# Scores of the last 32 tokens from gathered rows of expert_u, narrower score matmuls, and a rearranged end of the run, in one layer with product-key experts

## What is computed

```python
mix = token_mixer(x, w_in, sb_norm_w, ret_norm_w, w_out)
x = layer_norm(DEEPNORM_ALPHA * x + mix, ln1_w, ln1_b)
# experts: 8 heads, two lists of 128 keys each, the best 16 of 128*128 experts per head and token
expert_idx, gate = ...                         # (256, 8, 16)
u = jnp.take(expert_u, idx_b, axis=0)          # rows of 2048
act = gelu(einsum('thkd,td->thk', u, xb))      # one score per picked expert
v = jnp.take(expert_v, idx_b, axis=0)
ffn = einsum('thkd,thk->td', v, gate * act)
x = layer_norm(DEEPNORM_ALPHA * x + ffn, ln2_w, ln2_b)
```

## Time and profile before

| | before |
|---|---|
| median of 3 runs | 1876.7 us |
| the profiled execution | 1876.2 us |
| its span | 1874.4 us |
| TensorE busy | 1850.5 us, 99% |
| TensorE weight loads | 1572.4 us, 84% |
| VectorE busy | 1280.2 us, 68% |
| GpSimd busy | 1055.0 us, 56% |
| ScalarE busy | 1018.8 us, 54% |
| mean granted TensorE clock | 0.996 |

### The profile page before, as it was taken

The page is one execution under the profiler, slowest core; times in us unless marked ns, Lnnn a source line. Parts: engine busy times, 40 slices in busy tenths (PEclk is TensorE's granted clock), DMA queues, the critical chain, the costliest instruction groups (busy, mean ns, idle before and its releaser), DMA issues.

```text
span 1874.4 us, 30301 instructions
## 1 busy us (share of the span) xinstructions
PE 1850.5 (99%) x9326; PEld 1572.4 (84%) x9326; DVE 1280.2 (68%) x1886; ACT 1018.8 (54%) x1842; POOL 1055.0 (56%) x769
## 2 busy tenths in 40 slices
PE   9999999999999999999999999999999999999996
PEld 7888888888888888888888888887888888888885
DVE  4555676768565454555555557966898888888887
ACT  4455555545566565555555555555555555555553
POOL 0000231200488989788888887726888666665423
PEclk9999999999999999999999999999999999999998
DMA  7777776664655666788998888977999999999993
GB/s 246 236 240 224 230 239 204 184 204 160 217 170 181 194 186 203 200 192 196 246 230 195 194 192 273 294 232 259 360 390 359 391 338 358 395 375 370 378 341 91
DMA packets 202730, 476.42 MB, mean 254 GB/s; under 512 B 63504, under 2 KB 65744, under 8 KB 201840
## 3 DMA queue, kind: packets, MB, share of 16 engines
q1 hardware_dynamic: 131824, 391.56, 62.0%
q0 software_dynamic: 52416, 80.02, 15.8%
q10 hardware_dynamic: 18432, 4.20, 1.1%
HBM read 453.41 MB, written 21.07 MB: 253 GB/s over the span
## 4 chain that ended last, share of the span: by engine, by line
PE 96%; DVE 2%; DMA 1%; ACT 0%; POOL 0%; issue 0%; SPq 0%; ACTq 0%; DVEq 0%
PE ps L750 25%; PE ps L503 14%; PE ps L505 14%; PE ps L504 14%; PE ps L756 13%; PE ps L790 6%; PE ps L791 6%; PE ps L720 0%; DMA x_nat<-in_x 0%; PE ps L493 0%; DMA act_dram<-halves 0%; DVE stats L1779 0%; PE ps L554 0%; DVE ps L1776 0%; DVE y_out L1801 0%; DVE act_both L1263 0%
## 5 line engine op out<-in xcount | busy, mean ns | idle before, releaser
L750 PE MATMUL ps<-act_both,split_hi 128*128 128x512 f32 x2048 | 513.3, 393 | 0.0
L1059 ACT ACTIVATE split_hi<-raw 128x512 fp32r<-128x512 f32 x512 | 308.0, 625 | 292.2 <-PE ps L756 289.9
L750 PEld LDWEIGHTS ps<-act_both,split_hi 128*128 128x128 f32 x2048 | 368.6, 189 | 65.6
L1509 DVE TENSOR_TENSOR split_lo<-raw,split_hi 128x512 fp32r<-128x512 f32 x368 | 284.0, 788 | 201.7 <-ACT split_hi L1059 197.0
L1179 ACT ACTIVATE v_hi<-v_tile 128x1024 fp32r<-128x1024 f32 x248 | 263.2, 1062 | 254.4 <-PE ps L791 247.0
L1729 DVE TENSOR_TENSOR v_lo<-v_tile,v_hi 128x1024 fp32r<-128x1024 f32 x248 | 308.1, 1265 | 79.1 <-ACT v_hi L1179 78.9
L1250 DVE TENSOR_TENSOR split_lo<-raw,split_hi 128x512 fp32r<-128x512 f32 x304 | 232.5, 771 | 162.1 <-ACT split_hi L846 161.1
L846 ACT ACTIVATE split_hi<-raw 128x512 fp32r<-128x512 f32 x344 | 216.4, 631 | 226.7 <-PE ps L505 224.4
L1927 POOL DMA_INDIRECT gate_dram<-pick_n,places x192 | 300.3, 1564 | 59.4 <-issue 59.4
L1975 POOL DMA_INDIRECT rows<-in_expert_v,picked x128 | 208.4, 1629 | 189.3 <-DVE row_sum L1741 116.7
L756 PEld LDWEIGHTS ps<-act_both,split_lo 128*128 128x128 f32 x2048 | 279.6, 190 | 19.9
(11 more groups left out here) (206 smaller groups left out, 2131.8 us busy)
## 6 DMA issues: line engine op xcount, KB each, us to landing
raw<-in_expert_u SPq DMA_DIRECT2D x256, 512.0 KB
v_tile<-in_expert_v SPq DMA_DIRECT2D x256, 512.0 KB, 7.0
raw<-in_w_in SPq DMA_DIRECT2D x112, 512.0 KB
raw<-in_w_out SPq DMA_DIRECT2D x32, 512.0 KB
...
act_dram<-halves ACTq DMA_DIRECT2D x128, 32.0 KB
```

The source lines that it names most:

```text
L750: return nc.tensor.matmul(ps[:, bank, :], split_hi[:, q % SPLITS, i * P:(i + 1) * P], act_both[:, k, :, :].rearrange("p a t -> p (a t)"), ...
L1059: nc.scalar.activation(split_hi[:, q % SPLITS, :], raw[:, q // 2, q % 2, :], ACT.Copy).then_inc(hi_ready, 1)
L1509: vec.tensor_tensor(split_lo[:, q % SPLITS, :], raw[:, q // 2 % RAWS, q % 2, :], split_hi[:, q % SPLITS, :].bitcast(f32), ALU.subtract).th ...
```

## The change

Five things change together.

1. The last 32 tokens (`OWN`) leave the dense scores. The score matmuls run over `UT` = 224 columns: `wide` over 2 x 224, `narrow` over 224. `act_dram` keeps 32 columns.
2. Their scores come from gathered rows: 32 indirect DMAs (`load_u_row`), each bringing 128 rows of `expert_u` of 8 KB, into two slots that lie in the space of the later value units. GpSimd issues two before the scatter, then one after every sixth scatter from the 25th on, the last two after it. VectorE computes one row's dot product per pair in pairs 22 to 53, in two halves of 1024 columns (`dot`), each between the splits of that pair, against the tokens' own activations (`x1_own`, read back from DRAM by SP). ScalarE applies the gelu before pair 62; GpSimd moves the results into place (`move_dots`).
3. The value stage's picked rows come in one indirect DMA of 8 KB per row; the weighing moves from GpSimd to VectorE (`weigh`, `weigh_dots`).
4. `PREFETCH` goes from 30 to 55, with a wait for all dots before it, and `APPLIED_AHEAD` from 48 to 32.
5. The end of the run: the last two weight tiles are split early into buffers of their own (`wlast`), the DMA of `row_sum`'s half is issued by GpSimd, and the norms of PART are reordered between VectorE, ScalarE and GpSimd.

```diff
+OWN = HB // 2
+UT = DENSE + OWN
+DOT_SLOTS, DOT_AT = 2, 22
+DOTS = OWN * PKEYS // P
-PREFETCH = 30
+PREFETCH = 55
-APPLIED_AHEAD = 48
+APPLIED_AHEAD = 32
...
@@ SP
-            with sp.Fori(1, PREFETCH) as i:
+            with sp.Fori(1, DOT_AT - 1) as i:
                 u_pair(i)
-            sp.wait_ge(picked_in, 64)
+            sp.wait_ge(picked_in, 128)
             sp.wait_ge(topk_done, 2)
+            sp.wait_ge(x1_out, X1_OUT)
+            for g in range(4):
+                sp.dma_start(x1_own[OWN * g:OWN * g + OWN, :], x1_dram[P - OWN:P, PART, :]).then_inc(own_in, 16)
+            with sp.Fori(DOT_AT - 1, PREFETCH) as i:
+                u_pair(i)
+            sp.wait_ge(dot_used, 2 * DOTS)
...
@@ TensorE, wide and narrow
-                    return nc.tensor.matmul(ps[:, bank, :], split_hi[:, q % SPLITS, i * P:(i + 1) * P],
-                                            act_both[:, k, :, :].rearrange("p a t -> p (a t)"), start=k == 0,
-                                            stop=k == KT - 1)
+                    return nc.tensor.matmul(ps[:, bank, 0:2 * UT].rearrange("p (a t) -> p a t", a=2),
+                                            split_hi[:, q % SPLITS, i * P:(i + 1) * P], act_both[:, k, :, 0:UT],
+                                            start=k == 0, stop=k == KT - 1)
...
-                    return nc.tensor.matmul(ps[:, bank, 0:SEQ], split_lo[:, q % SPLITS, i * P:(i + 1) * P],
-                                            act_hi[:, k, :], start=False, stop=False)
+                    return nc.tensor.matmul(ps[:, bank, 0:UT], split_lo[:, q % SPLITS, i * P:(i + 1) * P],
+                                            act_hi[:, k, 0:UT], start=False, stop=False)
...
@@ ScalarE, before split_w(PAIRS - 2)
+            act.wait_ge(applied, PAIRS)
+            for i in range(2):
+                nc.scalar.activation(wlast[i][:, HID:HID + HB], wexp[:, NT - 2 + i, P:DENSE], ACT.Copy)
+                nc.scalar.activation(wlast[i][:, HI0:HI0 + DENSE], wexp[:, NT - 2 + i, 0:DENSE], ACT.Copy
+                                     ).then_inc(last_w_hi, 1)
...
@@ VectorE
+            def dot(j, slot, half):
+
+                cols = slice(half * UNIT, half * UNIT + UNIT)
+                part = u_slots[slot][:, cols]
+                vec.scalar_tensor_tensor(out=part, in0=part, scalar=1.0, in1=x1_own[:, cols], op0=ALU.mult, op1=ALU.mult,
+                                         accum_out=dots[:, half, bass.ds(j, 1)]).then_inc(dot_used, 1)
+
+            def u_pair(pair, parity, j=None):
 
                 for k in (2, 3):
                     split_two(pair, parity, k)
+                    if j is not None and k == 2:
+                        dve.wait_ge(u_row_in[parity], pair * 8 - (DOT_AT + parity) * 8 + 16)
+                        dot(j, parity, 0)
                 add_halves(pair, 0, 2 * parity)
                 for k in (4, 5):
                     split_two(pair, parity, k)
+                    if j is not None and k == 4:
+                        dot(j, parity, 1)
...
-                chain.add(vec.tensor_scalar(places_f[HB:P, 1, :], places_f[HB:P, 0, :], 2.0, 1.0, ALU.mult, ALU.add))
                 dve.wait_ge(v_chain, chain.n)
-                chain.step(vec.tensor_scalar(places_f[HB:P, 0, :], places_f[HB:P, 0, :], 2.0, None, ALU.mult))
...
             dve.wait_ge(x1_out, X1_OUT)
-            dve.wait_ge(picked_in, 64)
-            with dve.Fori(PAIRS_A // 2, PAIRS // 2 - 1) as i:
+            dve.wait_ge(picked_in, 128)
+            with dve.Fori(PAIRS_A // 2, DOT_AT // 2) as i:
                 for s in range(2):
                     u_pair(i * 2 + s, s)
+            dve.wait_ge(own_in, 64)
+            with dve.Fori(DOT_AT // 2, (DOT_AT + DOTS) // 2) as i:
+                for s in range(2):
+                    u_pair(i * 2 + s, s, i * 2 + (s - DOT_AT))
...
@@ VectorE, value stage
+            def weigh(k):
+
+                part = slice(k * W_GROUP, (k + 1) * W_GROUP)
+                dve.wait_ge(act_in[k % 2], 16 * W_GROUP * (k // 2 + 1))
+                for half in range(2):
+                    some = slice(half * HB, half * HB + OWN)
+                    vec.tensor_tensor(picked_w[some, part], picked_act[some, part], picked_gate[some, part], ALU.mult
+                                      ).then_inc(weight_ready, 1)
...
@@ VectorE, end
-            for q in range(2):
-                end_norm(PART, q)
             for q in range(1, 4):
                 summed(FULL, q)
             end_var(FULL)
+            end_norm(PART, 0)
             end_shift(FULL)
...
@@ GpSimd
+                    def load_u_row(j):
+
+                        if j >= DOT_SLOTS:
+                            pool.wait_ge(dot_used, 2 * (j - DOT_SLOTS) + 2)
+                        eng.indirect_dma_start(u_slots[j % DOT_SLOTS][:, :], None, u_v,
+                                               bass.IndirectOffsetOnAxis(ap=dot_rows[:, j:j + 1], axis=0)
+                                               ).then_inc(u_row_in[j % DOT_SLOTS], 16)
+
+                    def rows_at(h, b, k):
+
+                        n = h * sum(per_head) + b * TOPK + k - h * TOPK
+                        j = DOT_SLOTS + (n - 24) // 6
+                        return j if n >= 24 and n % 6 == 0 and j < DOTS else 0
+
...
+                            if rows_at(h, b, k):
+                                load_u_row(rows_at(h, b, k))
...
+                    for g in range(4):
+                        eng.dma_start(dot_rows[OWN * g:OWN * g + OWN, :],
+                                      places_u[P - OWN:P, 0, DOTS * g:DOTS * g + DOTS]).then_inc(picked_in, 16)
...
-                    pool.wait_ge(picked_in, 64)
+                    pool.wait_ge(picked_in, 128)
...
+                    for j in range(DOT_SLOTS):
+                        load_u_row(j)
...
+                    for j in range(DOT_SLOTS + (PH * sum(per_head) - 24) // 6, DOTS):
+                        load_u_row(j)
...
                     load_row(STEPS - 1)
+                    pool.wait_ge(row_used, STEPS)
+                    eng.dma_start(row_half[0:HB, :], row_sum[HB:P, :]).then_inc(half_moved, 16)
```

122 lines of the change are left out of this document (78 added, 44 removed).

## The result

The changed kernel takes 1938.5 us (median of 4 runs, 1930.5 to 1946.4) against 1876.6 us (1876.0 to 1881.9) of the kernel before measured beside it: a ratio of 1.032 with an interval of 1.028 to 1.037. The forecast was 1881 us in a range up to 1908; the result is 57.5 us slower than the forecast and lies outside the range. The profiled execution was the slowest of the four: it took 1946.4 us, 8 us over the median, its span is 1944.3 us and its mean granted clock 0.972.

What follows compares the result with a forecast made beforehand. The prediction took TensorE, 96% of the span, to bound the kernel. Score stage +8.9, value stage +2 and end -6.4 us made +4.5 on 1876.2: 1881 us, with a range of 1862 to 1908.

Steps and rivals of the forecast that it cites:

- what a matmul costs: Score stage: narrower matmuls at 0.202 us wide and 0.112 us narrow, so a pair takes 10.05 us instead of 11.18.
- Rival C: Score matmuls: under 256 columns a matmul is no longer a single pass, some 2400 us in all; chance 0.05.
- Pairs 0 to 17: Early score stage: GpSimd's eight low halves, 10.24 us, set the pace, so 16.7 us are gained instead of 20.
- the mechanism: Score stage: late u rows hold VectorE, then TensorE; value stage starts at 1280.6 us, 8.9 later than before.
- Rival A: Score stage: the u rows keep up and TensorE sets the pace, 1805 us in all; chance 0.06.
- The stall of pair 18: Score stage: VectorE's longer wait for picked_in costs TensorE about 1.5 us, hidden since the rows set the end.
- the length of a scatter: GpSimd in the score stage: 1.873 us per scatter, six 11.24, with a row's 1.65 a cycle of 12.9 us.
- Rival B: Score stage: VectorE's dots slow GpSimd's scatter stream, a cycle of 15.3 us and 1946 us in all; chance 0.09.
- the start: GpSimd in the score stage: DMAs begin about 739 us, first scatter at 753.3, row 2 follows at 800.1.
- gate products beside splits: GpSimd's gate products beside VectorE's splits: VectorE at 9.6 us per pair; with weighing charged +2 us, 0 to 6.
- value stage: Value stage: TensorE busy throughout, one row gather issue instead of two; weighing and gate products together charged +2 us.
- the end: End of the run: early last weights gain 5.1 us, moved norms 2.9, new waits cost 1.3; together -6.4 us.

Runs made afterwards that it cites:

- experiment 1: Changed kernel with a u row gathered after every fourth scatter instead of every sixth: 1877.8 us, ratio 0.999 to the kernel before.
- experiment 3: Changed kernel with the u rows gathered but no dots, SP waiting for the rows themselves before the tile of pair 55: 1895.2 us, ratio 1.008.
- experiment 2: Changed kernel without gathered u rows and without dots: 1837.5 us, ratio 0.976.
- 7: Changed kernel with VectorE's low-half splits from pair 18 on subtracting a bank of PSUM instead of SBUF: 1904.7 us, ratio 1.013.
- 8: Changed kernel with the tokens' own activations copied to PSUM, so each dot reads one operand from SBUF: 1923.5 us, ratio 1.024.
- experiment 6: Changed kernel with the softmax reciprocals in PSUM, one operand of the multiplication that took 11.56 us: 1945.2 us, ratio 1.034.
- experiment 9: Changed kernel with eight gate products before the value stage instead of 32, and the dots moved before them: 1922.2 us, ratio 1.023.
- experiment 11: Kernel before with part 5 of the change alone (early last weights, row_sum's half on GpSimd, reordered norms): 1876.1 us, ratio 0.9992.
- 10: Changed kernel with a row every fourth scatter, eight gate products ahead, dots moved before them, picked_in wait behind pair 21: 1835.2 us, ratio 0.974.
- 12: Changed kernel with rows every fourth scatter, eight gate products ahead, dots moved early and in PSUM, picked_in wait and activation load later: 1826.4 us, ratio 0.972.

## Why the prediction was wrong

**Right: what a matmul costs.** 10.09 us a pair against 10.05 to 10.1, and the narrow products are 0.110 us apart (taken: 0.112). Rival C, that they are no single pass, is refuted. Pairs 0 to 17 are not paced by GpSimd, though the forecast assumed it: its low halves come every 1.25 us when nothing interrupts them, eight in 10.0, and 16 of the 17 steps from pair 1 to pair 17 are 10.09. From the start of pair 0 to that of pair 18 it took 185.3 us where the forecast had 187.1.

**Right: the mechanism.** The rows are late, VectorE waits for them with the splits behind it, and TensorE with VectorE. Rival A, that the rows keep up, would have needed experiment 1's rhythm: even with nothing beside it GpSimd's cycle is 12.5 us (experiment 3). The stall of pair 18 was hidden, though it was 7.6 us and not the 1.5 of the text, and the falls of the clock behind gaps seem to have been hidden too: the rows set the pace at a clock of 0.89 as well.

**Wrong: the length of a scatter, 27.8 us of 65.4.** The step that failed is "A scatter takes 1.873 us, six take 11.24", the larger term of the cycle of 12.9 us: 1.873 was read from a stretch in which pairs take 11.18 us, and carried over unchanged to one where VectorE has dots in addition and the splits come in another rhythm. A scatter took 1.729 + 0.305 = 2.034 us from start to start. Six are 12.2 instead of 11.24, and a row 1.71 instead of 1.65: 13.9. Over 27 cycles the scatters are 26.1 us of this and the rows 1.6. Rival B named this mechanism and priced it at a cycle of 15.3; it gave it to the dots alone. That its 1946 us comes close to the measured time is luck: the cycle brought 27.8 of its 65 us, and the others came from terms that it doesn't have. Splits and dots share it: the mean is 1.709 us without dots (experiment 2), 1.641 with the splits' second operand in PSUM (7), 1.681 with the dots' (8). The bounds "12.5 to 13.5" were drawn around one row's uncertainty, that of the row issue, and left the larger term, six scatters, without any.

Why the same splits lengthened the scatters so little before is a matter of when they meet. A scatter is lengthened if a VectorE instruction with two SBUF operands is already running when it starts, by what that instruction has left, less 0.13 us. In the changed kernel 86 of the 192 scatters started so and took 1.938 us on average; the other 106 took 1.560, none over 1.58. The rows follow the same rule: 30 of 32 started under one and took 1.43 us, the other two 0.98. In the kernel before the splits that ran into a scatter's start in the steady stretch had only 0.18 us left and the scatter took 1.59 us; further on 0.23 us and 1.64. So 1.564 was the mean of a favourable phase that came with the rhythm of 11.18 us, and no price of a scatter.

**Wrong: the start, 8.6 us until row 2.** The first scatter was 3.4 us late. GpSimd's DMAs began at 744.3 us, not 739: VectorE made the places only when the low halves had ended (experiment 6), so GpSimd waited 3.5 us behind its last one instead of 0.8; and this execution had come to the score stage 2.9 us later (556.7 against 553.8 us), which hardly comes from the change, as that start lay between 553.3 and 556.0 in the experiments on the changed kernel. The DMAs and rows in front of the first scatter took 12.4 us instead of the 14.3 counted. The 25 scatters added 5.2, at 2.08 us each. Row 29 then landed and was used 9.5 us after its issue instead of 8, which is the rest of the 37.9.

**Wrong: gate products beside splits, 16 us.** "I charge +2 us" stood on 79.71 busy of 93 us in the earlier trace rows, 9.6 us a pair, "close to 10.1". Busy time of VectorE there holds waits for GpSimd, and these grow with how closely the splits follow each other: 1.16 us per split on average before, where they came with pauses, and 1.51 in the changed kernel, where VectorE was behind and ran them without one. Eight of these with two additions come to 12.9 us, over 10.1. An engine at 95% of its limit was treated as one with 5% to spare.

Of the 18.5 us between row 29's dot and the value stage some 2 are left without a cause.

**Wrong: value stage, 5.4 us at its start instead of 2.** The first picked row is gathered after the products. The first eighth of the value products lasts 81.1 us, before it was 75.7, and in experiment 9, with fewer products ahead, 74.4.

**Wrong: the end, -0.8 instead of -6.4.** (This is what is left of the 9.0 us.) "No idle gap before the held products": experiment 11 shows what is late next. The forecast followed only the instruction that had been late and not the other one that meets GpSimd's addition. The span ended 15.5 us after the start of the last product against 14.0, in experiment 11 after 13.7, and in experiments 9, 10 and 12 only after 17.9 to 18.1: what of this is the stores' is not settled.

**What could have been seen.** The earlier trace rows has the same issue at 0.97 and 1.90 us, and the earlier trace rows a scatter of 2.23 us beside splits. Both were read, and the rival built on them got a chance of 0.09.
